# First attention of a two-block transformer kernel: probabilities turned on VectorE, values as 32-row tiles

## The chip, the cores and the metric

The kernel runs on one NeuronCore of one Trainium2 chip. The metric is the time of the whole program in device microseconds, smaller is better. TensorE is written PE in the rows, VectorE DVE, ScalarE ACT, GpSimd POOL, SyncE SP.

## What is computed

Two transformer blocks over 512 tokens of width 1024, all in float32. The change lies in the mixer of the first block: sixteen query heads in two groups of eight, each group with one key and value head of width 64, over a band of two blocks of 128 tokens, with a learned sink in each softmax. Its output is gated, added to a gated pooling mixer, and projected.

```python
def swa_sink_attention(q, k, v, sinks):
    qb = q.reshape(B, nb, BLOCK, N_KV_HEADS, GQA_GROUP, HEAD_DIM)     # nb = 4 blocks of 128
    kb, vb = band(k), band(v)                                         # the block before and the block itself
    s = jnp.einsum('bnqhgd,bnkhd->bhgnqk', qb, kb, ...)
    s = jnp.where(mask, s, -jnp.inf)
    m = jnp.maximum(jnp.max(s, axis=-1, keepdims=True), sink)
    p = jnp.exp(s - m)
    denom = jnp.sum(p, axis=-1, keepdims=True) + jnp.exp(sink - m)
    probs = (p / denom).astype(v.dtype)
    out = jnp.einsum('bhgnqk,bnkhd->bnqhgd', probs, vb)
...
        a = pool_mixer(u_pool, w_pool[l], pool_scale[l])
        b = swa_sink_attention(q, k, v, sinks[l])
        x = x + (g_pool * a + g_attn * b) @ w_out[l]
```

The mask leaves the 128 keys up to each query. The first block of 128 queries has no block before it, so it needs only 128 keys; the other three need 256.

## The kernel before

Activations lie transposed, features on the 128 partitions and tokens along the free axis. All weights come as one stream of units, each 1024 x 128. SyncE loads a unit into one of two `raw` buffers; GpSimd splits it into a high part and a low part in the fp32r format (`split`, L486 and L494; a few high parts are made by ScalarE, `weight_high`). Four pairs of buffers `w_hi`, `w_lo` go round. A tile of a projection (`tile`, L1102) is 24 matmuls of 128 x 128 weights by 512 tokens: eight key tiles, three products each (high by high, high by low, low by high). A buffer is free again when its unit's tile is done (`unit_done`). Each engine runs its own program in order; semaphores tie them together.

The first block goes: input projections of the pooling part, K and V, Q; then the attention loop, into which the 16 gate projections are woven; then the output projection (`U_OUT`, eight units); then the feed-forward part.

V arrives transposed in `vT` and is turned by four TensorE transposes (L1251) in round t = 3 of the Q projections, into `vtok` (tokens on partitions). In that stage VectorE scales each tile (`scaled_in`, L1915) and applies the rotation (`qk`), and last_window and window_parts of the pooling part stand between.

The attention loop has 16 steps n. Step n handles four heads of block `blk = n // 4`; two successive steps make up the eight heads of group `g = n // 2 % 2`. The work of a step:

- TensorE: `scores(n + 2)` (L1283, two 64-row tiles side by side, into PSUM banks 2 and 3), `turn(n)` (L1293, profiled under the helper's line L1167: 128 x 128 transposes of the probabilities), `gate(n + 2)` (one projection tile, L1102), `values(n)` (L1303, two column tiles of 64 side by side).
- VectorE: `scaled_in` of the gate tile (L1915), `masked_max(n + 2)` (L2025 to L2040: adds the mask, reduces, takes in the sink), `normalise(n + 1)` (L2048 to L2052: adds the sink's share, reciprocal, multiplies the probabilities), `attn_out` for every second step (L2067: multiplies the values' result by the gate), `gate_pool` from step 7 (L2058).
- ScalarE (all its operations are recorded at L581): `turned(n)` copies the transposed probabilities from PSUM to `pT`, `gate(n + 1)` takes tanh of the gate tile, `exps(n + 2)` exponentiates the four heads and sums them.

So the softmax of a step is made two steps ahead, and TensorE covers it with the gate tile. The last two steps have no gate tile.

After the loop VectorE adds pooling and attention (`mixed`, L2101), ScalarE makes the high part (`high(1, REAL)`) and VectorE the low part (L1852) into `h_hi5` and `h_lo5`, one key tile after the other. TensorE takes the first two tiles of the output projection together by key tile (`tile_pair`, L1121), then five single tiles (L1102), then the last in two halves of 256 tokens (`tile_sides`, L1176). VectorE adds each finished tile to the residual (L2123).

`gbuf` is the memory of `g_hi` and `g_lo`, which the pooling part uses up to `pooled(1)` and the feed-forward part uses later.

Of the kernel before, what the change touches and what calls it, by code (L numbers as in the profile page):

```python
# [17 lines left out]
P = 128  # L18
# [7 lines left out]
T = 512  # L26
# [111 lines left out]
def build(nc, w_stream, w_ba, x_t, vec, cst, cst1, cst2, pos, out):  # L138
    ctx = ExitStack()
    with ctx:  # L140
# [58 lines left out]
        vtok = ar(NB, P)  # L199
# [4 lines left out]
        vT_r = arena_r[:, ar.at:ar.at + T]  # L204
        vT = ar(T)
# [5 lines left out]
        GA = arena[:, mid:mid + 8 * T].rearrange("p (a b) -> p a b", b=T)  # L211
        ar.at = mid + 8 * T
        sm_r = [arena_r[:, ar.at + 1024 * n:ar.at + 1024 * (n + 1)].rearrange("p (a b) -> p a b", b=256) for n in range(2)]
        sm = [ar(4, 256), ar(4, 256)]
        pT = ar(2, 512)
# [43 lines left out]
        def area(x, *shape):  # L259
# [58 lines left out]
            "s_ready s_read mx_ready exp_ready p_ready pT_ready pT_copied pv_done o_read "  # L318
# [51 lines left out]
        def sum_banks(d):  # L370

            return (0, 0, 0, 0, 2, 4, 0, 2)[d]

# [203 lines left out]
        def _(act):  # L577
# [83 lines left out]
            a(vT, ps[:, 1, :], ACT.Copy).then_inc(S["tile_read"], 1)  # L661
            weight_high(13)
            for t in range(1, 9):
# [20 lines left out]
            def gate(i):  # L684
                act.wait_ge(S["in_scaled"], 10 + i + 1)
                if i == 0:
                    act.wait_ge(S["qk_dve"], 9)
                    act.wait_ge(S["v_turned"], 1)
# [12 lines left out]
            def exps(n):  # L701
                s = sm[n % 2] if n >= 4 else sm[n % 2][:, :, P:2 * P]
# [382 lines left out]
        def _(pe):  # L1085
# [8 lines left out]
            def tile(u, i, dst, pieces=None):  # L1094

                a_hi, a_lo = (h_hi, h_lo) if pieces else (h_hi5, h_lo5)
# [72 lines left out]
            def tile_sides(u, banks, between=None):  # L1169

                pe.wait_ge(split_done[u % 4], rounds(u))
                hi, lo = w_hi[u % 4], w_lo[u % 4]
                for c, side in enumerate(sides):
                    for k in range(KT):
                        for n, (w, h) in enumerate(((hi, h_hi5), (hi, h_lo5), (lo, h_hi5))):
# [66 lines left out]
            for t in range(1, 9):  # L1242
                pe.wait_ge(S["tile_read"], t + 8)
                tile(U_Q + t - 1, 0, [ps[:, (9 + t) % 2, :]])
                if t == 3:
# [4 lines left out]
                    for b in range(NB):  # L1250
                        last = turned_into(ps[:, 7, b * P:(b + 1) * P], vT_r[:, b * P:(b + 1) * P])  # L1251
# [22 lines left out]
            def scores(n):  # L1274
                blk, g, half = n // 4, n // 2 % 2, n % 2
# [11 lines left out]
            def turn(n):  # L1287
                blk = n // 4
                pe.wait_ge(S["p_ready"], n + 1)
                wait(pe, S["pT_copied"], n)  # L1290
                for kb in range(0 if blk else 1, 2):
                    for m in range(4):
                        last = turned_into(ps[:, 4 + kb, m * P:(m + 1) * P], sm_r[n % 2][:, m, kb * P:(kb + 1) * P])  # L1293
                last.then_inc(S["pT_ready"], 1)

            def values(n):
                blk, g, half = n // 4, n // 2 % 2, n % 2
                pe.wait_ge(S["pT_copied"], n + 1)
                wait(pe, S["o_read"], n // 2 - 1)
                kbs = range(0 if blk else 1, 2)  # L1300
                for kb in kbs:
                    for par in range(2):
# [1333 lines left out]
```

## Time and profile before

| | |
|---|---|
| time, median of 3 runs | 1422.29 us (1421.27 to 1424.07) |
| span of the profiled execution | 1420.3 us |
| TensorE busy | 1364.4 us, 96% |
| VectorE busy | 712.4 us, 50% |
| ScalarE busy | 442.0 us, 31% |
| GpSimd busy | 903.1 us, 64% |
| attention loop | about 140 to 270 us of the span |

The median lies 2.0 us over the span of the profiled execution. A record of a matmul lasts longer than its share of the engine, since matmuls overlap; the time between two starts is what one costs. A float32 matmul leaves two records, an fp32r matmul one. "idle before" names the wait ahead of an instruction and what released it. The granted clock (PEclk) is a share of 2.4 GHz.

### The profile page before, as it was taken

The numbers are of one execution on the slowest core, as the hardware profiler recorded it, in microseconds if no ns is written. First come the engines' busy times: TensorE is split into PE (matmuls) and PEld (weight loads), VectorE is DVE, ScalarE is ACT, GpSimd is POOL, SyncE is SP. The second block draws the span as 40 slices with busy tenths as digits, with TensorE's granted clock in tenths as the row PEclk, the third lists the DMA queues.
The fourth block names the chain that finished last, engine by engine and source line by source line (L and its number), as shares of the span: only waits on it lengthen the run. The fifth ranks groups of instructions, "written<-read, shape, count | busy, mean of one in ns | idle before, by whom it ended". The sixth has DMA issues, their size and how long they took to land. (4 is left out here: it accounts for less than half of the span.)

```text
span 1420.3 us, 20890 instructions
## 1 busy us (share of the span) xinstructions
PE 1364.4 (96%) x7495; PEld 1113.6 (78%) x7495; DVE 712.4 (50%) x1147; ACT 442.0 (31%) x888; POOL 903.1 (64%) x1043
## 2 busy tenths in 40 slices
PE   7999999999999999999899999889989999999996
PEld 5877777688888888888778886649788888888884
DVE  7888767744444445113578875685554111211113
ACT  3344544422212122111345445634433111111111
POOL 6856655377777777876465753414367767687772
PEclk9999999999999999999999999999999999999998
DMA  5321311133323232322121111000022332233221
GB/s 195 107 87 60 105 60 60 45 104 107 103 89 103 89 103 89 104 91 101 45 78 57 48 59 60 16 1 2 30 89 82 111 97 95 89 104 99 93 89 60
DMA packets 31888, 113.78 MB, mean 80 GB/s; under 512 B 3536, under 2 KB 3920, under 8 KB 31696
## 3 DMA queue, kind: packets, MB, share of 16 engines
q1 hardware_dynamic: 31680, 112.72, 24.1%
q8 instruction: 43, 0.70, 0.2%
q14 instruction: 21, 0.17, 0.0%
q10 hardware_dynamic: 144, 0.18, 0.0%
HBM read 110.79 MB, written 2.10 MB: 79 GB/s over the span
## 5 line engine op out<-in xcount | busy, mean ns | idle before, releaser
L494 POOL TENSOR_TENSOR w_lo<-raw,w_hi 128x256 fp32r<-128x256 f32 (+1 forms) x804 | 649.7, 838 | 42.4 <-ACT w_hi L581 26.5
L486 POOL TENSOR_SCALAR w_hi<-raw 128x1024 fp32r<-128x1024 f32 (+1 forms) x188 | 202.6, 1078 | 382.9 <-issue 340.8
L1102 PE MATMUL ps<-h_hi,w_hi 128*128 128x512 f32 x912 | 362.0, 397 | 0.8 <-POOL w_lo L494 0.7
L1102 PE MATMUL ps<-h_lo,w_hi 128*128 128x512 f32 x912 | 355.2, 390 | 0.0
L1102 PE MATMUL ps<-h_hi,w_lo 128*128 128x512 f32 x912 | 355.1, 389 | 0.0
L1102 PEld LDWEIGHTS ps<-h_hi,w_hi 128*128 128x128 f32 x912 | 171.2, 188 | 40.3 <-issue 3.2
L1102 PEld LDWEIGHTS ps<-h_lo,w_hi 128*128 128x128 f32 x912 | 171.2, 188 | 37.7 <-issue 3.0
L1102 PEld LDWEIGHTS ps<-h_hi,w_lo 128*128 128x128 f32 x912 | 171.2, 188 | 35.9
L581 ACT ACTIVATE arena<-ps 128x512 f32<-128x512 f32 (+6 forms) x194 | 90.4, 501 | 228.0 <-PE ps L1167 74.7
L581 ACT ACTIVATE arena<-arena 128x512 f32<-128x512 f32 (+6 forms) x194 | 102.4, 531 | 174.7 <-DVE arena L2552 119.2
L2166 DVE TENSOR_TENSOR g_lo<-arena,g_hi 128x512 fp32r<-128x512 f32 x54 | 47.0, 879 | 210.6 <-ACT g_hi L581 210.6
L1365 PE MATMUL ps<-g_hi,w_hi 128*128 128x512 f32 x368 | 143.2, 389 | 0.0
L1365 PE MATMUL ps<-g_lo,w_hi 128*128 128x512 f32 x368 | 143.2, 389 | 0.0
L1365 PE MATMUL ps<-g_hi,w_lo 128*128 128x512 f32 x368 | 143.2, 389 | 0.0
L581 ACT ACTIVATE arena<-ps,V 128x512 f32<-128x512 f32 (+2 forms) x115 | 80.8, 720 | 198.8 <-DVE ps L2150 128.8
L581 ACT ACTIVATE g_hi<-arena 128x512 fp32r (+1 forms) x54 | 33.4, 630 | 217.1 <-PE ps L1365 201.8
L2552 DVE SCALAR_TENSOR_TENSOR arena<-ps,arena 128x512 f32<-128x512 f32 x32 | 21.7, 690 | 119.9 <-PE ps L1102 113.7
L1365 PEld LDWEIGHTS ps<-g_hi,w_lo 128*128 128x128 f32 x368 | 69.1, 188 | 14.4
L1365 PEld LDWEIGHTS ps<-g_lo,w_hi 128*128 128x128 f32 x368 | 69.1, 188 | 14.4
L1365 PEld LDWEIGHTS ps<-g_hi,w_hi 128*128 128x128 f32 x368 | 69.1, 188 | 14.3
L2150 DVE TENSOR_TENSOR ps<-ps,arena 128x512 f32<-128x512 f32 x33 | 23.1, 699 | 102.1 <-PE ps L1102 102.1
L2298 DVE SCALAR_TENSOR_TENSOR arena<-arena,V 128x528 f32<-128x528 f32 x48 | 53.8, 1121 | 16.2 <-ACT arena L581 14.7
(308 smaller groups left out, 1989.8 us busy)
## 6 DMA issues: line engine op xcount, KB each, us to landing
raw<-in_w_stream SPq DMA_DIRECT2D x204, 512.0 KB, 3.4
out<-xT SPq DMA_DIRECT2D x8, 256.0 KB, 2.0
xT<-in_x_t SPq DMA_DIRECT2D x1, 1056.0 KB, 8.1
xT<-in_x_t SPq DMA_DIRECT2D x1, 792.0 KB, 6.0
arena<-in_cst SPq DMA_DIRECT2D x1, 528.0 KB, 4.4
C<-in_cst SPq DMA_DIRECT2D x1, 448.0 KB, 9.4
xT<-in_x_t SPq DMA_DIRECT2D x1, 264.0 KB, 3.7
arena<-in_pos SPq DMA_DIRECT2D x1, 256.0 KB, 3.6
```

The source lines that it names most:

```text
L486: pool.tensor_scalar(w_hi[j][:, k0:KT, :], raw[j % 2][:, k0:KT, :], 1.0, 1.0, ALU.mult, ALU.mult).then_inc(S["pool_step"], 1)
L494: low = pool.tensor_tensor(w_lo[j][:, k:k + n, :], raw[j % 2][:, k:k + n, :], w_hi[j][:, k:k + n, :], ALU.subtract)
L581: return nc.scalar.activation(o, i, f, **kw)
L1102: last = mm(dst[p], w[:, k, :], h[:, k, cols], start=(k == 0 and n == 0), stop=(k == KT - 1 and n == 2))
L1365: last = mm(ps[:, f, :], w[:, f, :], h[:, j, :], start=(start and n == 0), stop=(stop and n == 2), skip_group_check=True)
L2150: v.tensor_tensor(ps[:, q + 1, :], ps[:, q + 1, :], n_ri[:, 0:T], ALU.mult).then_inc(S["up_scaled"], 1)
L2166: v.tensor_tensor(g_lo[:, j, :], src[:, ds(4 * i + j), :].rearrange("p a b -> p (a b)"), g_hi[:, j, :], ALU.subtract).then_inc(S["ms_ready ...
L2298: ins = v.scalar_tensor_tensor(out=y5, in0=x5[:, d % 2, j:j + L], scalar=vcol("dconv", 12 * j + d), in1=y5, op0=ALU.mult, op1=ALU.add)
L2552: v.scalar_tensor_tensor(out=rb[:, q, :], in0=ps[:, bank, :], scalar=0.0, in1=n_ri[:, 0:T], op0=ALU.max, op1=ALU.mult).then_inc(S["relu_re ...
```

## The change

In words:

- Order: step n now handles group `n // 8`, block `n // 2 % 4`, half `n % 2` (`head_step`): first all four blocks of the first eight heads, then those of the second.
- V is written by ScalarE four times over (`vT` gets 2048 elements a partition), turned by sixteen TensorE transposes, four in each of the rounds t = 3 to 6, and copied to `vrep` in four pieces. So each strip of 32 partitions holds all values of 32 keys.
- The normalising multiplication moves from VectorE to ScalarE (`normalised`, four scaled copies); VectorE keeps the denominators.
- The probabilities are no longer turned by TensorE and copied by ScalarE. VectorE turns them in 32 x 32 blocks into `p_turned` (in `gbuf`).
- `values(k)` works on two steps at once: up to 64 matmuls of 32 rows by 64 columns with 128 moving columns, into PSUM banks 4 to 7, one bank for each strip of 32 queries. `attn_out(k)` reads the four banks with four instructions.
- `mixed` and its high and low part for key tiles 0 to 3 move into the loop (steps 10 to 14); high parts go over `GA` (`GA_r`), low parts over `U` (`U_r`), no longer to `h_hi5` and `h_lo5`.
- The output projection takes three tiles together (`out_three`), first key tiles 0 to 3, then `values(7)`, then key tiles 4 to 7; four single tiles and the last one in halves follow, with banks `f % 4`.

```diff
@@ ACT, rounds of the Q projections
-                    act.wait_ge(S["v_turned"], 1)
-                    a(vtok.rearrange("p a b -> p (a b)"), ps[:, 7, :], ACT.Copy).then_inc(S["v_ready"], 1)
+                if 3 <= t < 7:
+                    act.wait_ge(S["v_turned"], t - 2)
+                    a(vrep[:, 4 * (t - 3):4 * (t - 2), :].rearrange("p a b -> p (a b)"), ps[:, 7, :], ACT.Copy).then_inc(S["v_ready"], 1)
@@ ACT, attention loop
-            def turned(n):
-                act.wait_ge(S["pT_ready"], n + 1)
-                wait(act, S["pv_done"], n)
-                if n >= 4:
-                    a(pT[:, 0, :], ps[:, 4, :], ACT.Copy)
-                a(pT[:, 1, :], ps[:, 5, :], ACT.Copy).then_inc(S["pT_copied"], 1)
+            def normalised(n):
+                s = sm[n % 2] if head_step(n)[1] else sm[n % 2][:, :, P:2 * P]
+                act.wait_ge(S["den_ready"], n + 1)
+                b = 16 * (n % 2)
+                for m in range(4):
+                    last = a(s[:, m, :], s[:, m, :], ACT.Copy, scale=small[:, b + 8 + m:b + 9 + m])
+                last.then_inc(S["p_ready"], 1)
+
+            def mixed_high(f):
+                act.wait_ge(S["hn_ready"], f + 1)
+                a(GA_r[:, f, :], n_h[:, f % 2, 0:T], ACT.Copy).then_inc(S["hi_ready"], 1)
 
             exps(0)
             pooled_out(1)
             for n in range(16):
-                turned(n)
+                normalised(n)
                 if n == 0:
                     exps(1)
                 if 1 <= n < 15:
                     gate(n + 1)
+                if 11 <= n < 15:
+                    mixed_high(n - 11)
                 if n < 14:
                     exps(n + 2)
-            high(1, REAL)
+            for f in range(4, KT):
+                mixed_high(f)
@@ PE, attention loop
-            def values(n):
...
+            def values(k):
+
+                g, blk, _ = head_step(2 * k)
+                pe.wait_ge(S["pt_ready"], 2 * k + 2)
+                wait(pe, S["o_read"], k)
+                for kb in range(0 if blk else 4, 8):
+                    for c in range(4):
+                        for par in range(2):
+                            last = mm(ps[64 * par:64 * par + 64, 4 + c, 0:P], vrep[q32(c), 4 * (blk - 1) + kb, 64 * g:64 * g + 64],
+                                      p_turned[q32(c), k % 2, :, 2 * par:2 * par + 2, 32 * kb:32 * kb + 32],
+                                      start=(kb == (0 if blk else 4)), stop=(kb == 7))
+                last.then_inc(S["pv_done"], 1)
@@
             for n in range(16):
                 if n < 14:
                     scores(n + 2)
-                turn(n)
-                if n < 14:
                     gate(n + 2)
-                if n == 0:
+                if n == 1:
                     pe.wait_ge(S["pm_read"], 8)
-                values(n)
+                if n % 2 and n < 15:
+                    values(n // 2)
             pe.wait_ge(S["tile_read"], 34)
-            tile_pair(U_OUT, 1, [[ps[:, 0, :]], [ps[:, 1, :]]])
...
+            pe.wait_ge(S["s_read"], 16)
...
+            out_three(range(4))
+            values(7)
+            out_three(range(4, KT))
@@ DVE, attention loop
-            def normalise(n):
+            def denominators(n):
                 b = 16 * (n % 2)
-                lo = 0 if n >= 4 else P
-                s = sm[n % 2][:, :, lo:256]
                 dve.wait_ge(S["exp_ready"], n + 1)
                 den = small[:, b + 8:b + 12]
                 step(v.tensor_tensor(den, den, small[:, b + 12:b + 16], ALU.add))
                 step.settle()
-                step(v.reciprocal(den, den))
-                step.settle()
-                v.tensor_tensor(s, s, den.unsqueeze(2).to_broadcast([P, 4, 256 - lo]), ALU.mult).then_inc(S["p_ready"], 1)
+                v.reciprocal(den, den).then_inc(S["den_ready"], 1)
+
+            def turn(n):
+
+                g, blk, half = head_step(n)
+                lo = 0 if blk else P
+                dve.wait_ge(S["p_ready"], n + 1)
+                wait(dve, S["pv_done"], n // 2 - 1)
+                if n == 0:
+                    product(dve, U_PM + 1)
+                v.transpose(p_turned[:, n // 2 % 2, half, :, lo:256], sm[n % 2][:, :, lo:256]).then_inc(S["pt_ready"], 1)
@@
+            def attn_out(k):
+
+                g, blk, _ = head_step(2 * k)
+                dve.wait_ge(S["pv_done"], k + 1)
+                dve.wait_ge(S["tile_read"], 18 + 4 * g + 4)
+                for c in range(4):
+                    c0 = blk * P + 32 * c
+                    ga = GA[:, 4 * g:4 * g + 4, c0:c0 + 32]
+                    ins = v.scalar_tensor_tensor(out=ga, in0=ga, scalar=1.0, in1=ps[:, 4 + c, 0:P].rearrange("p (a b) -> p a b", b=32),
+                                                 op0=ALU.add, op1=ALU.mult)
+                ins.then_inc(S["o_read"], 1)
@@
             masked_max(0)
-            normalise(0)
+            denominators(0)
             masked_max(1)
             for n in range(16):
+                turn(n)
                 if 1 <= n < 15:
                     scaled_in(U_GATE + n + 1, (n + 1) % 2)
-                if n == 6:
-                    attn_out(3)
+                if n % 2 == 0 and 2 <= n < 15:
+                    attn_out(n // 2 - 1)
                 if n < 14:
                     masked_max(n + 2)
                 if n < 15:
-                    normalise(n + 1)
...
+                    denominators(n + 1)
                 if 7 <= n < 15:
                     gate_pool(n - 7)
...
+                if 10 <= n < 14:
+                    mixed(n - 10)
+                if 11 <= n < 15:
+                    mixed_low(n - 11)
+            attn_out(7)
+            for f in range(4, KT):
+                mixed(f)
+                if f > 4:
+                    mixed_low(f - 1)
+            mixed_low(KT - 1)
```

## Rows read from the trace of the kernel before

**Rows 1.** Stages: us from:to, length, busy us of each engine, PEclk, DMA share, GB/s

```profile
180.00:220.00 40.00, 39.76 (x224) 29.47 (x222) 28.80 (x50) 18.65 (x60) 18.74 (x23) 1.00 0.21 66
266.00:268.00 2.00, 0.88 (x8) 0.74 (x8) 1.97 (x4) 1.02 (x3) 0.61 (x1) 0.97 0.08 8
268.00:270.00 2.00, 1.88 (x8) 0.77 (x8) 1.83 (x4) 1.15 (x3) 0.00 (x0) 0.50 0.64 254
270.00:272.00 2.00, 2.00 (x8) 1.65 (x7) 1.97 (x5) 0.63 (x1) 0.00 (x0) 0.67 0.00 0
```

**Rows 2.** TensorE timeline, one step with 256 keys: start us, duration us, engine, line

```profile
227.32 1.08 PE L1303 MATMUL ps<-arena 128*64 128x256 f32 x8
228.33 1.13 PE L1283 MATMUL ps<-arena 64*128 64x256 f32 x8
229.40 0.88 PE L1167 MATMUL ps<-ident_r,arena_r 128*128 128x128 f32 x8
230.12 0.47 PE L1102 MATMUL ps<-h_hi,w_hi 128*128 128x512 f32 x1
...
235.74 1.08 PE L1303 MATMUL ps<-arena 128*64 128x256 f32 x8
```

**Rows 3.** TensorE timeline, values and transposes of a step with 128 keys

```profile
161.66 0.65 PE L1303 MATMUL ps<-arena 128*64 128x256 f32 x4
162.25 1.13 PE L1283 MATMUL ps<-arena 64*128 64x256 f32 x8
163.31 0.53 PE L1167 MATMUL ps<-ident_r,arena_r 128*128 128x128 f32 x4
```

**Rows 4.** TensorE timeline, end of the loop and start of the output projection

```profile
264.09 1.08 PE L1303 MATMUL ps<-arena 128*64 128x256 f32 x8 [1.17 <-ACT arena L581]
266.07 0.88 PE L1167 MATMUL ps<-ident_r,arena_r 128*128 128x128 f32 x8 [0.89 <-DVE arena L2052]
268.12 1.98 PE L1303 MATMUL ps<-arena 128*64 128x256 f32 x8 [1.17 <-ACT arena L581]
270.03 0.80 PE L1121 MATMUL ps<-h_hi,w_hi 128*128 128x512 f32 x1
...
281.92 0.50 PE L1102 MATMUL ps<-h_hi,w_hi 128*128 128x512 f32 x1
```

**Rows 5.** TensorE: second attention's values (timeline), and 32x32 matmuls by line

```profile
806.22 1.46 PE L1496 MATMUL ps<-arena 128*64 128x128 f32 x20
...
L1666 PE MATMUL ps<-arena,hbuf x128: 191/191/212, 953.9 to 955.1; 32*32 32x32 f32 x128
```

**Rows 6.** VectorE timeline: scaled_in, masked_max from its first to its last instruction

```profile
213.02 0.69 DVE L1915 TENSOR_TENSOR ps<-ps,arena 128x512 f32<-128x512 f32 x1
213.62 1.21 DVE L2025 TENSOR_TENSOR arena<-ps,band 128x1024 f32<-128x1024 f32 x1
...
216.52 0.16 DVE L2040 TENSOR_TENSOR arena<-arena,V 128x4 f32<-128x4 f32 x1
```

**Rows 7.** ScalarE timeline: pooled_out(1), first and last of exps, eight scaled copies

```profile
146.31 2.43 ACT L581 ACTIVATE arena<-ps,V 128x512 f32<-128x512 f32 x4 [1.87 <-PE ps L1265]
...
216.71 0.51 ACT L581 ACTIVATE arena<-arena 128x256 f32<-128x256 f32 x1 [1.58 <-DVE arena L2040]
...
218.70 0.19 ACT L581 ACTIVATE arena<-arena 128x4 f32<-128x4 f32 x1
...
312.33 3.31 ACT L581 ACTIVATE h_hi<-xT,V 128x256 fp32r<-128x256 f32 x8 [1.52 <-PE ps L1176]
```

**Rows 8.** VectorE by line: duration ns min/median/max of transposes; a PSUM copy, mean ns

```profile
L2372 DVE STREAM_TRANSPOSE arena<-hbuf x4: 692/702/707, 918.1 to 920.3; 32x512 f32<-32x512 f32 x4
...
L2380 DVE STREAM_TRANSPOSE arena<-arena x1: 2081/2081/2081, 921.3 to 921.3; 128x1024 f32<-128x1024 f32 x1
...
L2292 DVE COPY arena<-ps 128x128 f32<-128x128 f32 x16 | 4.6, 286 | 0.4 <-PE ps L1496 0.4
```

**Rows 9.** V's transposes on TensorE, and VectorE's wait in round 7

```profile
87.09 0.86 PE L1167 MATMUL ps<-ident_r,arena_r 128*128 128x128 f32 x4
87.79 1.09 PE L1235 MATMUL ps<-arena,C 128*128 128x512 f32 x2
...
113.40 0.70 DVE L1915 TENSOR_TENSOR ps<-ps,arena 128x512 f32<-128x512 f32 x1 [0.39 <-PE ps L1102]
```

More of the change, by code:

```diff
@@ L203, in build @@
         W0, W1 = ar(2, L), ar(2, L)
-        vT_r = arena_r[:, ar.at:ar.at + T]
-        vT = ar(T)
+        vT, vT_r = (x[:, AC - 4 * L:AC - 4 * L + 16 * P].rearrange("p (b c k) -> p b c k", c=4, k=32) for x in (arena, arena_r))
         sqb, qgb = ar(2, T), ar(2, T)
@@ L1092, in unit, with tile @@
                 last.then_inc(unit_done[u % 4], 1)
-            def tile(u, i, dst, pieces=None):
-                a_hi, a_lo = (h_hi, h_lo) if pieces else (h_hi5, h_lo5)
+            def tile(u, i, dst, parts=None, pieces=None):
+                a_hi, a_lo = parts or ((h_hi, h_lo) if pieces else (h_hi5, h_lo5))
                 def work(hi, lo):
@@ L1249, in _ @@
                     pe.wait_ge(S["tile_read"], 10)
-                    for b in range(NB):
-                        last = turned_into(ps[:, 7, b * P:(b + 1) * P], vT_r[:, b * P:(b + 1) * P])
+                if 3 <= t < 7:
+                    wait(pe, S["v_ready"], t - 3)
+                    for b in range(4):
+                        last = turned_into(ps[:, 7, b * P:(b + 1) * P], vT_r[:, 4 * (t - 3) + b, :, :].rearrange("p c k -> p (c k)"))
                     last.then_inc(S["v_turned"], 1)
@@ L1285, in scores @@
                 last.then_inc(S["s_ready"], 1)
[L1287 to L1294, printed above, removed]
-            def values(n):
[L1297 to L1302, printed above, removed]
-                        last = mm(ps[64 * par:64 * par + 64, 6 + n // 2 % 2, 256 * half:256 * half + 256],
-                                  vtok[:, blk - 1 + kb, 64 * g:64 * g + 64], pT[:, kb, 256 * par:256 * par + 256],
-                                  start=(kb == kbs[0]), stop=(kb == 1))
+            def values(k):
[8 more added lines that the diff above has]
+                                      start=(kb == (0 if blk else 4)), stop=(kb == 7))
                 last.then_inc(S["pv_done"], 1)
@@ L1323, in _, with out_three @@
                     scores(n + 2)
-                turn(n)
-                if n < 14:
                     gate(n + 2)
-                if n == 0:
+                if n == 1:
                     pe.wait_ge(S["pm_read"], 8)
-                values(n)
+                if n % 2 and n < 15:
+                    values(n // 2)
             pe.wait_ge(S["tile_read"], 34)
-            tile_pair(U_OUT, 1, [[ps[:, 0, :]], [ps[:, 1, :]]])
-            for f in range(1, KT):
-                if f > 1:
-                    pe.wait_ge(S["x_ready"], f - 1)
-                if 1 < f < KT - 1:
-                    tile(U_OUT + f, 0, [ps[:, f % 2, :]])
-            tile_sides(U_OUT + KT - 1, (1, 3))
+            pe.wait_ge(S["s_read"], 16)
+            def out_three(ks):
+                for k in ks:
+                    pe.wait_ge(S["h_ready"], parts_before(1) + k + 1)
+                    for e in range(3):
+                        if k == 0:
+                            pe.wait_ge(split_done[(U_OUT + e) % 4], rounds(U_OUT + e))
+                        hi, lo = w_hi[(U_OUT + e) % 4], w_lo[(U_OUT + e) % 4]
+                        for m, (w, x) in enumerate(((hi, GA_r[:, k, :]), (hi, U_r[:, k, REAL]), (lo, GA_r[:, k, :]))):
+                            last = mm(ps[:, e, :], w[:, k, :], x, start=(k == 0 and m == 0), stop=(k == KT - 1 and m == 2))
+                        if k == KT - 1:
+                            last.then_inc(unit_done[(U_OUT + e) % 4], 1)
+            out_three(range(4))
+            values(7)
+            out_three(range(4, KT))
+            for f in range(3, KT):
+                wait(pe, S["x_ready"], f - 3)
+                if f < KT - 1:
+                    tile(U_OUT + f, 0, [ps[:, f % 4, :]], (GA_r, U_r[:, :, REAL]))
+            pe.wait_ge(S["x_ready"], KT - 2)
+            tile_sides(U_OUT + KT - 1, (1, 3), (GA_r, U_r[:, :, REAL]))
             def up(i):
@@ L1426, in wide @@
                     pe.wait_ge(S["bat_ready"], 2)
-                tile(u, 0, [ps[:, 2 * (n % 2), :]], [REAL])
+                tile(u, 0, [ps[:, 2 * (n % 2), :]], pieces=[REAL])
             def k2_side(t):
@@ L2018, in masked_max @@
             def masked_max(n):
+                g, blk, half = head_step(n)
                 b = 16 * (n % 2)
-                lo = 0 if n >= 4 else P
+                lo = 0 if blk else P
                 s = sm[n % 2][:, :, lo:256]
                 dve.wait_ge(S["s_ready"], n + 1)
-                wait(dve, S["pT_ready"], n - 1)
+                wait(dve, S["pt_ready"], n - 1)
                 m = band[:, lo:256].unsqueeze(1).to_broadcast([P, 4, 256 - lo])
```

72 lines of the change are left out of this document (31 added, 41 removed).

## The prediction

> **What bounds the kernel now.** I read the page first (TensorE 96% of the span), then the stages. In 180 to 220 us TensorE is busy 39.76 of 40 us, VectorE 28.80, ScalarE 18.65 [rows 1]: TensorE sets the pace of the attention loop. The TensorE timeline of one step (four heads, 256 keys) gives its period: values at 227.32, scores at 228.33, transposes at 229.40, the gate tile from 230.12, the next values at 235.74 [rows 2]. That is 8.42 us: values 1.01, scores 1.07, transposes 0.72, gate 5.62. In a step with 128 keys the values take 0.59 (161.66 to 162.25), and I take half, 0.37, for its transposes [rows 3]. At the end no gate tile is left to cover the softmax: three waits of 1.17, 0.89 and 1.17 us, the last values take 1.91 us instead of 1.01, and the output projection starts at 270.03 [rows 4]. Its first pair of tiles ends at 281.92, and six tiles of 5.44 us (24 matmuls of 0.227) follow.
>
> The question is what the period of a step becomes when TensorE sheds work and the other two engines get an order of their own.
>
> **Part 1, TensorE's own work.** Gone: the transposes, 12 x 0.72 + 4 x 0.37 = 10.1 us, and the values, 12 x 1.01 + 4 x 0.59 = 14.5 us. New: eight values blocks, six of 64 matmuls and two of 32, each matmul 32 rows x 64 columns with 128 moving columns. The nearest size is second attention's values: 10 matmuls of 128 columns in 1.46 us, two column tiles side by side; less 0.16 for the last one's way out, 0.26 us for one tile's matmul [rows 5]. With eight tiles side by side, 64 matmuls are eight such slots, 2.1 us; no concurrency beyond two gives 64 x 0.13 = 8.3 us. The nearest in concurrency are the 32x32 matmuls: 128 records (64 matmuls) start within 1.1 us, four tiles at a time [rows 5]. The diff's order (four row strips, two column halves, then the next key block) names eight different tiles in a row, so I take 2.2 us (1.2 for the half block). TensorE alone would then need 2 x (1.07 + 5.62) + 2.2 = 15.6 us for two steps, not 16.84.
>
> Those records start some 9 ns apart. The Trainium skill says in TensorE: Matmul & The Clock Gate, Wait — 56ns, not 53.3ns?, that start to start never drops below about 25 ns; by that the 128 records of a block would take 3.2 us, 1.0 us over my figure. The trace disagrees, at least for 32x32 tiles.
>
> **Part 2, the loop of VectorE and ScalarE.** This carries the forecast. ScalarE's new order is normalised(n), gate(n+1), exps(n+2); VectorE's is turn(n), scaled_in(n+1), attn_out, masked_max(n+2), denominators(n+1). So turn(n+1) waits for normalised(n+1), which stands on ScalarE behind exps(n+2), which waits for masked_max(n+2), which stands on VectorE behind turn(n). Each step runs this whole ring, and nothing in it overlaps:
> masked_max 3.06 us (213.62 to 216.68) [rows 6]; exps 2.18 (216.71 to 218.89) [rows 7]; normalised, four scaled copies of 256 columns, by the row of eight such copies in 3.31 us 0.40 each and 0.10 at the end, 1.70 [rows 7]; turn 1.16; scaled_in 0.60 (213.02 to 213.62) [rows 6]; three handoffs of 0.03. The transpose of 1024 elements is bounded by 2.08 us (strided on both sides) and by 0.70 for 512 with runs of 32; the diff's reads and writes are contiguous, nearest to the second, which makes 1.24 with 0.08 overlapped [rows 8]. Sum 8.79 us. Every second step adds attn_out, four instructions of 128 elements at 0.29 [rows 8] less overlap: 0.85. Two steps take 18.4 us, against 16.84 now and TensorE's own 15.6. TensorE waits some 2.8 us in every two steps, and VectorE becomes part of the bound though it is busy less than TensorE. gate_pool, mixed, mixed_low and the denominators lie in VectorE's wait for ScalarE (3.9 us): nothing. gate and mixed_high lie on ScalarE beside masked_max: nothing. A slower values block is covered up to those 2.8 us in two steps.
>
> The walk. turn(0) comes after pooled_out(1) (146.31 + 2.43 [rows 7]) and a normalised of 128 columns (1.26, an estimate: 0.11 less for each copy): 150.0. Up to turn(15) the ring holds: masked_max 2 to 15, 12 x 3.06 + 2 x 1.86 = 40.4; exps, 12 x 2.18 + 2 x 1.74 = 29.7; normalised 1 to 15, 12 x 1.70 + 3 x 1.26 = 24.2; turns 0 to 14, 11 x 1.16 + 4 x 0.62 = 15.2; scaled_in 14 x 0.60 = 8.4; attn_out 7 x 0.85 = 6.0; the first attn_out waits 0.6 for gate 3; the last denominators 0.4; handoffs 1.3. Together 126.2 (the half sizes 1.86, 1.74 and 0.62 are the same rows at half the elements). turn(15) starts at 276.2.
>
> **Part 3, the tail.** The output projection now takes three tiles together, and its first half (key tiles 0 to 3) only waits for gate 15 and its reader: turn(14) + 2.4 us, or 273.8. Before it TensorE idles some 7 us, since after values(6) it has no work. 36 matmuls, 8.16 us, to 281.9; values(7) 2.2, to 284.1; attn_out 0.85, mixed 0.60, the high part 0.63, the low part 0.69 and handoffs 0.13, to 287.0; 36 matmuls more, to 295.2. Before, three tiles were done at 281.92 + 5.44 = 287.36 [rows 4]. So +7.8 us. The five tiles that follow have the old price; POOL's splits for them (3.9 us each) begin when the first of the three tiles is done and stay ahead of 5.44 us tiles.
>
> **Part 4, turning the values earlier.** Sixteen transposes instead of four: three batches more, each up to 0.70 us (87.09 to 87.79) and at least 0.37 [rows 9]. VectorE waits for TensorE's tile in that stage up to the seventh round (0.39 us at 113.40) [rows 9], so a later tile is passed on: 0 to 2.1, I take +1.6. ScalarE's wider copy of V (2048 elements) and three copies more lie in its waits of 3 us a round: nothing.
>
> **Part 5, the clock.** At 266 to 268 the granted clock is 0.97 and at 268 to 270 it is 0.50 (1.2 GHz), right after the three waits, and 0.67 in the next 2 us [rows 1]; the last values and the first projection matmuls pay for it. The old fall cost 0.9 us in the values (1.91 against 1.01 [rows 2, 4]) and 1.0 in the pair (11.89 us for 48 matmuls against 10.88), 1.9 together. The wait of 7 us before the projection is longer than those three together, so I count one fall at 1.9. The wait of 2.9 us before the second half may bring another, 0 to 1.9: half of it. Falls inside the loop are covered by the 2.8 us. Sum +2.9.
>
> **The sum.** +7.8 + 1.6 + 2.9 = +12.3 us. The profiled execution has a span of 1420.3, the median is 2.0 over it: 1432.6 in the profile, 1434.6 in the median.
>
> **The rivals.**
> A, faster: TensorE stays the bound. For it: VectorE (28.80) and ScalarE (18.65) have room in 40 us [rows 1]. Then -10.1 - 14.5 + (6 x 2.2 + 2 x 1.2) = -9.0, the three waits -3.2, the slow clock -1.9, Part 4 +1.6: -12.5, 1409.8. It decides as soon as the ring takes less than 7.8 us a step instead of 9.2. Against it: none of the ring's terms is shorter in any row, and the order is in the diff. 0.09.
> B, the transposes take 2.08 us: 11 x 0.84 + 4 x 0.33 = +10.6 more, 1445. 0.12.
> C, the change doesn't do what it says: the 32-row tiles don't overlap beyond the two column halves. Two steps then take 13.4 + 8.3 = 21.7 us on TensorE, 3.3 over the ring, five times, and 6 more in the last block: about +22 more, 1457. At four tiles side by side (4.2 us) the loop still hides it and the last block adds 2.0. 0.07.
> D, within 0.2% (1419.4 to 1425.1; about the least that a measurement tells from no change): the clock never falls, the transposes of V are hidden and attn_out's four instructions cost as much as the old one: +7.8 - 2.5 = +5.3, still 1427.6. It would need 2.5 us more than that. 0.03.
>
> **How the numbers follow.** Forecast 0.69, A 0.09, B 0.12, C 0.07, D 0.03. Ends of the forecast: low +5.3 with 0.5 off for faster values, 1427; high: V turned +0.5, clock +1.0, attn_out 4 x 0.29 +2.2, values at 3.4 us +1.2: 1439.5. B is taken in up to 1446 and the room between: 1427 to 1446 holds 0.81. Faster 0.09, same 0.03, slower 0.88.
>
> **What would show it.** After: VectorE's transposes of 1024 elements at about 1.24 us and each following a ScalarE copy; waits on VectorE for ScalarE of 2 to 3.5 us a step; waits on ScalarE for the masked maximum; two steps 18.4 us apart; TensorE's share in the loop near 85%; values blocks of 2.2 us; a TensorE wait of 7 us before the projection with the clock at 0.50 behind it. I am wrong if TensorE has no waits in the loop (A), if the transposes are near 2 us (B) or a values block above 4 us (C).

## The result, and the profile after

The changed kernel takes 1447.54 us (median of 4 runs, 1442.41 to 1448.68) against 1422.95 us before (4 runs, 1421.27 to 1424.07): a ratio of 1.0173, with a 95% interval of 1.0160 to 1.0186. The forecast was 1434.6 us with a range up to 1446.0. The direction was right, the size was half of what came: +12.3 us forecast, +24.6 us measured. The profiled execution of after has a span of 1445.5 us, where the sum said 1432.6.

First the stages, as in [rows 1]: us from:to, length, busy us of each engine, granted clock, DMA share, GB/s.

```profile
180.00:220.00 40.00, 35.61 (x422) 27.79 (x428) 25.29 (x46) 18.16 (x58) 15.96 (x21) 0.98 0.18 54
284.00:288.00 4.00, 2.31 (x6) 1.83 (x7) 3.35 (x11) 2.80 (x6) 0.00 (x0) 0.50 0.00 0
288.00:292.00 4.00, 4.00 (x13) 3.22 (x12) 1.03 (x1) 0.00 (x0) 0.00 (x0) 0.65 0.00 0
300.00:304.00 4.00, 2.22 (x5) 1.82 (x6) 3.64 (x7) 1.86 (x3) 0.00 (x0) 0.63 0.00 0
304.00:308.00 4.00, 4.00 (x11) 3.05 (x10) 1.27 (x2) 1.92 (x2) 0.00 (x0) 0.51 0.01 4
```

TensorE, 39.76 of 40 us busy in the loop before, is busy 35.61 now. What it waits for (engine, line, waited for, us in total, times, longest), in 100 to 320 us of after:

```profile
PE ps L1299 <- DVE arena L2050: 13.8, 8, 3.4
PE ps L1349 <- ACT arena L584: 8.3, 1, 8.3
PE ps L1349 <- DVE arena_r L2114: 3.1, 1, 3.1
PE ps L1311 <- DVE gbuf L2083: 2.9, 4, 1.5
```

The scores wait for masked_max (L2050 is its first instruction), the values for the turning (L2083), the projection for gate 15 and then for the low part of the fifth key tile. VectorE waits in its turn for ScalarE:

```profile
DVE gbuf L2083 <- ACT arena L584: 38.4, 15, 3.6
```

The parts of the forecast, by line on VectorE (count | busy us, mean ns | idle before), and the values blocks and the tail in TensorE's timeline (start, duration):

```profile
L2083 DVE STREAM_TRANSPOSE gbuf<-arena 128x1024 f32<-128x1024 f32 x12 | 15.0, 1246 | 31.2 <-ACT arena L584 31.2
L2063 DVE TENSOR_SCALAR arena<-arena 128x4 f32<-128x4 f32 x16 | 7.3, 456 | 0.5
L2061 DVE TENSOR_TENSOR arena<-arena,V 128x4 f32<-128x4 f32 x16 | 6.9, 430 | 0.5
L2065 DVE TENSOR_TENSOR arena<-arena,V 128x4 f32<-128x4 f32 x16 | 5.5, 342 | 0.5
```

```profile
202.28 2.10 PE L1311 MATMUL ps<-gbuf,arena 32*64 32x128 f32 x128 [1.46 <-DVE gbuf L2083]
204.31 0.72 PE L1299 MATMUL ps<-arena 64*128 64x128 f32 x8
...
285.69 1.22 PE L1349 MATMUL ps<-arena_r,w_hi 128*128 128x512 f32 x2 [8.28 <-ACT arena L584]
...
296.53 2.10 PE L1311 MATMUL ps<-gbuf,arena 32*64 32x128 f32 x128
...
301.78 1.22 PE L1349 MATMUL ps<-arena_r,w_hi 128*128 128x512 f32 x2 [3.14 <-DVE arena_r L2114]
...
312.99 0.62 PE L1115 MATMUL ps<-arena_r,w_hi 128*128 128x512 f32 x2
```

Here stand the transpose at 1.246 us (forecast 1.24), the values block at 2.03 us from start to start of what follows (2.2), the wait before the projection at 8.28 us (7) with the clock at 0.50 behind it, and the second wait at 3.14 us (2.9). Three projection tiles are done at 312.99; before they were done at 287.36 [rows 4]. That is 25.6 us of shift, so the whole loss lies ahead of this point.

What the forecast did not have is in the three groups of 128x4 instructions. Each takes 0.16 to 0.17 us when nothing disturbs it, and 0.34 to 0.46 us on the mean here. One step of after shows how. VectorE:

```profile
192.75 1.21 DVE L2050 TENSOR_TENSOR arena<-ps,band 128x1024 f32<-128x1024 f32 x1
193.99 1.22 DVE L2053 TENSOR_REDUCE arena<-arena 128x4 f32<-128x1024 f32 x1
195.25 0.50 DVE L2061 TENSOR_TENSOR arena<-arena,V 128x4 f32<-128x4 f32 x1
195.78 0.67 DVE L2063 TENSOR_SCALAR arena<-arena 128x4 f32<-128x4 f32 x1
196.49 0.65 DVE L2065 TENSOR_TENSOR arena<-arena,V 128x4 f32<-128x4 f32 x1
```

and GpSimd at the same time:

```profile
193.87 1.04 POOL L489 TENSOR_SCALAR w_hi<-raw 128x1024 fp32r<-128x1024 f32 x1 [4.82 <-issue]
195.00 2.82 POOL L497 TENSOR_TENSOR w_lo<-raw,w_hi 128x256 fp32r<-128x256 f32 x4
```

GpSimd splits the next weights in five instructions of 0.70 to 1.04 us. A small VectorE instruction that falls among them ends about when the running GpSimd instruction does. masked_max takes 4.4 us here (192.75 to 197.14) instead of the 3.06 of [rows 6]. The add from PSUM and the reduction beside it keep their 1.21 and 1.22 us. Two full steps, from one turning to the next but one, take 18.9 to 20.2 us, where the forecast had 18.4.

### The profile page after: what moved, and what is told of

Its sections match the earlier page's. It is cut to its first block and busy times, and to the rows that moved or that the text cites. A ratio compares the mean times of both kernels' runs of the same rounds, so it can differ in the third digit from the quotient of the medians.

```text
span 1445.5 us, 22303 instructions
## 1 busy us (share of the span) xinstructions
PE 1365.9 (94%) x8179; PEld 1118.1 (77%) x8179; DVE 717.7 (50%) x1171; ACT 454.0 (31%) x927; POOL 897.6 (62%) x1043
## 5 line engine op out<-in xcount | busy, mean ns | idle before, releaser
L1115 PE MATMUL ps<-h_hi,w_hi 128*128 128x512 f32 x872 | 348.4, 400 | 1.1 <-POOL w_lo L497 1.1
L1115 PE MATMUL ps<-h_lo,w_hi 128*128 128x512 f32 x872 | 341.1, 391 | 0.0
L1115 PE MATMUL ps<-h_hi,w_lo 128*128 128x512 f32 x872 | 340.9, 391 | 0.0
L1115 PEld LDWEIGHTS ps<-h_hi,w_hi 128*128 128x128 f32 x872 | 164.6, 189 | 43.4 <-issue 7.5
L1115 PEld LDWEIGHTS ps<-h_lo,w_hi 128*128 128x128 f32 x872 | 164.6, 189 | 36.7 <-issue 3.0
L1115 PEld LDWEIGHTS ps<-h_hi,w_lo 128*128 128x128 f32 x872 | 164.6, 189 | 34.5
L584 ACT ACTIVATE arena<-arena 128x256 f32<-128x256 f32 (+5 forms) x258 | 126.5, 516 | 192.2 <-DVE arena L2588 119.2
L584 ACT ACTIVATE arena<-ps 128x512 f32<-128x512 f32 (+6 forms) x169 | 77.9, 494 | 187.3 <-PE ps L1180 37.6
L2334 DVE SCALAR_TENSOR_TENSOR arena<-arena,V 128x528 f32<-128x528 f32 x48 | 53.7, 1120 | 16.1 <-ACT arena L584 14.7
```

Of the source, the lines that this page charges most:

```text
L584: return nc.scalar.activation(o, i, f, **kw)
L1115: last = mm(dst[p], w[:, k, :], h[:, k, cols], start=(k == 0 and n == 0), stop=(k == KT - 1 and n == 2))
L2334: ins = v.scalar_tensor_tensor(out=y5, in0=x5[:, d % 2, j:j + L], scalar=vcol("dconv", 12 * j + d), in1=y5, op0=ALU.mult, op1=ALU.add)
```

## The experiments

The theory: the loop is set by the circle of Part 2 (turn, masked_max, exps, normalised, turn), and it is longer than forecast because GpSimd's split stretches the small instructions of masked_max, which are part of the circle. Rivals: TensorE itself is slower than its rows of work say (32-row tiles, clock); the split has nothing to do with it; the tail is more than forecast for a reason of its own.

**e1_den_first: the circle cut by order alone**

```diff
 # ScalarE
+            normalised(0)
+            exps(1)
             for n in range(16):
-                normalised(n)
-                if n == 0:
-                    exps(1)
                 if 1 <= n < 15:
                     gate(n + 1)
+                if n < 15:
+                    normalised(n + 1)
...
 # VectorE
+                if n < 15:
+                    denominators(n + 1)
                 if n < 14:
                     masked_max(n + 2)
-                if n < 15:
-                    denominators(n + 1)
```

> One edit of order in the kernel after, nothing else: VectorE makes denominators(n+1) before masked_max(n+2) instead of behind it, and ScalarE does normalised(n+1) before exps(n+2). The probabilities of step n+1 are then ready before VectorE is through with masked_max(n+2), and the circle turn(n), masked_max(n+2), exps(n+2), normalised(n+1), turn(n+1) is cut. Theory (the loop is set by this circle, and TensorE waits for it): a step falls from 9.0 us to TensorE's own 7.7 to 7.8 us, the VectorE waits for ScalarE ahead of the turning (38 us in all) nearly vanish, the first half of the out projection starts 15 to 22 us earlier than its 285.7 us, and the whole comes to about 1428 us (1421 to 1434). Rival (TensorE itself is slower with the 32-row blocks, by tiles that do not overlap or by the clock): the order of the two vector engines changes nothing on TensorE, and the time stays at 1445 to 1449 us.

Measured: 1415.82 us, ratio to before 0.9954 (0.9940 to 0.9968). That is 31.7 us less than after, 5 us below the range that was expected, and faster than the kernel before. Its loop, from the stages:

```profile
180.00:220.00 40.00, 40.00 (x432) 31.57 (x431) 32.13 (x66) 24.54 (x82) 20.42 (x27) 1.00 0.21 67
```

TensorE is busy 40.00 of 40 us; the first half of the projection starts at 255.50 instead of 285.69, behind 0.81 us of waiting instead of 8.28. No work was taken away: the small instructions of masked_max are still stretched, to 0.27 to 0.29 us on the mean, and the denominators' add to 0.51. The order alone had cost 31.7 us, and the rival in which TensorE's own work is the cause is out. The profiled executions are 34.8 us apart. 27.1 of that lie between turn(0) and turn(15) (107.88 us instead of 134.93), 5.4 in the tail, where 2.3 and 1.4 us are a clock that falls less, 1.5 ahead of turn(0), where the clock of after had fallen and that of e1_den_first had not, and 0.8 behind the three tiles.

**e4_split_small: GpSimd's part in the circle**

```diff
-            rep(pool, U_UP // 4, split, HIGH_ROUNDS)
+            rep(pool, 9, lambda i: split(i, None, P if isinstance(i, int) else 4), HIGH_ROUNDS)
+            with pool.Fori(9, U_UP // 4, 1) as i:
+                split(i)
 # in split(i, held, w): the operands become w_hi[j][..., 0:w], raw[...][..., 0:w], w_lo[j][..., 0:w]
```

The kernel leaves out most of the split weights of 14 gate units.

> The kernel after, with GpSimd's weight split in weight units 20 to 35 cut to 4 of 128 columns of each tile (the rest of the split weights of 14 gate units are left out, so most of the gates' products are not the reference's); every wait and every other instruction stays. Theory (the circle is stretched by the small VectorE instructions of masked_max, which take 0.5 to 1.0 us instead of 0.16 while GpSimd's split runs): the groups of 128x4 instructions fall from 0.43, 0.46, 0.34 and 0.22 us to 0.16 us, a step falls from 9.0 to 9.2 us to the forecast's 8.5 to 8.8, and the whole to about 1438.5 us (1436 to 1442), which is 9 us below the kernel after and still above the kernel before. Rival (the stretch is not GpSimd's, or lies off the path): 1445 to 1449 us.

Measured: 1433.88 us, ratio 1.0087 (1.0070 to 1.0104), 13.7 us less than after and 2 us below the range that was expected. The run is its own control, since the full split comes back at 234.5 us. Without it (VectorE's timeline; line 2052 is the first instruction of masked_max, 2063 to 2067 are its small ones, 2085 is the turning):

```profile
183.23 1.25 DVE L2085 STREAM_TRANSPOSE gbuf<-arena 128x1024 f32<-128x1024 f32 x1 [3.55 <-ACT arena L586]
...
185.76 1.21 DVE L2052 TENSOR_TENSOR arena<-ps,band 128x1024 f32<-128x1024 f32 x1
...
188.66 0.16 DVE L2067 TENSOR_TENSOR arena<-arena,V 128x4 f32<-128x4 f32 x1
...
201.29 1.25 DVE L2085 STREAM_TRANSPOSE gbuf<-arena 128x1024 f32<-128x1024 f32 x1 [3.55 <-ACT arena L586]
```

and with it:

```profile
242.46 1.25 DVE L2085 STREAM_TRANSPOSE gbuf<-arena 128x1024 f32<-128x1024 f32 x1 [2.37 <-ACT arena L586]
...
244.21 1.21 DVE L2052 TENSOR_TENSOR arena<-ps,band 128x1024 f32<-128x1024 f32 x1
...
246.90 0.65 DVE L2065 TENSOR_SCALAR arena<-arena 128x4 f32<-128x4 f32 x1
247.59 0.64 DVE L2067 TENSOR_TENSOR arena<-arena,V 128x4 f32<-128x4 f32 x1
...
261.92 1.25 DVE L2085 STREAM_TRANSPOSE gbuf<-arena 128x1024 f32<-128x1024 f32 x1 [1.76 <-ACT arena L586]
```

masked_max takes 3.06 us in the first (185.76 to 188.82) and 4.02 in the second. Two steps, from turning to turning, take 18.06 us in the first (183.23 to 201.29; forecast 18.4) and 19.46 us in the second (242.46 to 261.92).

Not all of the gain is the circle's. The two profiled executions are 16.1 us apart: 4.05 us ahead of turn(0) (148.80 against 152.85), 7.55 between turn(0) and turn(15) (127.38 against 134.93), 3.64 from there to the three tiles, 0.9 behind them. Of the first 4.05, some 1.5 are the early fall of the clock in after. The 3.64 are the clock alone. Behind a second wait of 3.15 us it does not fall at all here:

```profile
289.34 0.74 PE L1351 MATMUL ps<-arena_r,w_hi 128*128 128x512 f32 x2 [3.15 <-DVE arena_r L2116]
...
297.75 0.62 PE L1117 MATMUL ps<-arena_r,w_hi 128*128 128x512 f32 x2
```

That is 8.41 us for the second half of the three tiles against 11.21 in after, and the first half takes 10.01 us against 10.84. So GpSimd's part in the circle is 7.6 us, and that the whole comes within 1 us of the forecast of 1434.6 is in part luck.

**e11_tail_split_small: the same cut where the circle is cut too** (its base, e5_tail, follows below)

> The kernel e5_tail with the same cut of GpSimd's split as in e4_split_small (weight units 20 to 35 are split in 4 of 128 columns only; the rest is left out, so most of the gates' products are not the reference's). The same cut took 13.7 us off the kernel after. Theory (the stretched small instructions cost time only as members of the circle): with the circle cut they lie beside TensorE's work, and at most the 1 to 3 us ahead of the loop, where TensorE waits 0.9 us for VectorE, can come back: 1409 us (1406.5 to 1411). Rival (the split slows the loop in some other way as well, through TensorE's weights or the loads): 1397 to 1401 us.

Measured: 1407.88 us, ratio 0.9902 (0.9879 to 0.9924), 2.6 us less than e5_tail. The small instructions of masked_max fall to 0.16 to 0.17 us as well, and next to nothing comes of it: turn(0) starts 2.6 us earlier (148.76 against 151.38), and from there to turn(15) it is 107.13 us against 106.94 in e5_tail. In this loop the contention costs time only through the circle.

**e8_values_twice and e9_tail_values_twice: who has slack**

```diff
-                for kb in range(0 if blk else 4, 8):
+                for kb in 2 * list(range(0 if blk else 4, 8)):
```

The same line was changed in the kernel after and in e5_tail.

> The kernel after, with each block of values multiplied twice over (the second pass starts the sums anew): TensorE has 2.05 us more work per pair of steps (1.2 us at the two half-size blocks), 14 to 15 us in all eight blocks. Theory (the loop waits for the circle through VectorE and ScalarE, and TensorE has 2 to 3 us of idle time in each pair of steps there): the seven blocks inside the loop cost next to nothing, values(7) stands on the path and costs its 2.05 us; the whole comes to 1449.5 us (1448 to 1453). Rival (TensorE sets the pace): 1461 to 1463 us.

> The kernel e5_tail with each block of values multiplied twice over, the same addition that cost the kernel after nothing. Theory (with the circle cut TensorE sets the pace of the loop): the 14 us of added matmuls come out in full, 1424 us (1421 to 1426). Rival (VectorE, 80 to 90% busy there, sets the pace and TensorE has slack): 1411 to 1415 us.

Measured: after with doubled values 1445.30 us (ratio 1.0154, 1.0135 to 1.0173), not slower than after and below the range expected; e5_tail with doubled values 1428.54 us (1.0047, 1.0029 to 1.0065), 18.1 us slower than e5_tail and above the range expected. The added matmuls are 12.4 us and not the 14 of the expectations: a block of 64 matmuls grows from 2.03 to 3.80 us, one of 32 from 1.14 to 2.03. In after those within the loop are free (turn(0) to turn(15) 135.17 us against 134.93), and the wait of 8.28 us before the projection shrinks to 4.83. values(7), behind the loop, is not free: it brings its 1.8 us and a gap of 1.17. The clock gives that back, since the second half takes 9.71 us instead of 11.21 and the early fall is missing (turn(0) starts at 151.20 instead of 152.85). Once the circle is cut, the added matmuls cost their full time. What lies above that comes at least in part with gaps in and behind the doubled streams, for which the profile names nothing that TensorE waits for (the waits of e9_tail_values_twice; the scores have 2.5 us of the same kind, and e8_values_twice has 5.7 us in all):

```profile
PE ps L1312 <- issue: 3.6, 3, 1.4
```

How much of the median they make is open, for the profiled execution of e9_tail_values_twice is the slowest of its four, 4.8 us above the median.

**e6_fill: the clock behind the first wait**

```diff
-            pe.wait_ge(S["tile_read"], 34)
             pe.wait_ge(S["s_read"], 16)
+            for _ in range(34):
+                mm(ps[:, 3, :], ident_r[:], h_hi5[:, 0, :], start=True, stop=True)
+            pe.wait_ge(S["tile_read"], 34)
```

> The kernel after, with 34 matmuls of 128x512 (7.7 us) into an unused PSUM bank where TensorE waits 8.3 us for the last gate ahead of the out projection; nothing else is changed. Theory (after the wait the first half of the out projection runs at a granted clock of 0.50 to 0.65 and takes 10.8 us instead of 8.3): with the wait filled the clock stays at 1.00, the first half takes 8.3 to 8.5 us and the whole comes to 1445 us (1443.5 to 1446.5); the fall after the second wait (3.1 us) stays. Rival (the fall comes whatever TensorE did before, or only moves): 1447 to 1448 us and a first half of 10.8 us.

Measured: 1445.58 us, ratio 1.0160 (1.0141 to 1.0178), 2.0 us less than after. The two intervals overlap, so the times alone do not show a gain. The trace is clear:

```profile
277.36 8.00 PE L1339 MATMUL ps<-h_hi,ident_r 128*128 128x512 f32 x34
285.30 0.73 PE L1351 MATMUL ps<-arena_r,w_hi 128*128 128x512 f32 x2
...
293.80 2.10 PE L1311 MATMUL ps<-gbuf,arena 32*64 32x128 f32 x128
```

The first half takes 8.50 us (285.30 to 293.80) at a granted clock of 1.00, against 10.84 in after (285.69 to 296.53) at 0.50 and 0.65.

**e10_tail_alone and e5_tail: the second wait**

```diff
 # TensorE
-            out_three(range(4))
+            out_three(range(2))
             values(7)
-            out_three(range(4, KT))
+            out_three(range(2, KT))
...
 # VectorE
-                turn(n)
+                if n < 15:
+                    turn(n)
...
+                if n == 14:
+                    turn(15)
                 if 7 <= n < 15:
                     gate_pool(n - 7)
```

> The kernel after with the tail's edit alone (turn(15) ahead of the gate and mixing work of VectorE's step 14, values(7) behind the second key tile), the order of the loop as in the kernel after. Theory (in the kernel after the wait of 3.1 us between the halves and the clock of 0.63 and 0.51 behind it are the price of the tail's order, apart from the circle in the loop): both go, worth 3.1 us and 1.5 to 2.5 us, and the whole comes to 1442.5 us (1441 to 1444.5); the first half still starts behind a wait of 8 us and at a clock near 0.50. Rival (turn(15) is now waited for by VectorE, so that the gates and parts behind it come later and the gain is used up): 1446 to 1449 us.

> The kernel e1_den_first, with turn(15) put ahead of the gate and mixing work of VectorE's step 14 and values(7) put behind the second key tile of the out projection's first half instead of behind the fourth. Theory (the wait of 3.1 us between the halves stands because attn_out(7), mixed(4) and mixed_low(4) can only start once values(7) is through, and the granted clock of 0.61 behind it costs 1.2 us more): VectorE does these three beside key tiles 2 and 3, no wait and no fall are left, and the whole comes to 1411.5 us (1409.5 to 1413.5), some 4.3 us below e1_den_first. Rival (another wait takes its place, at values(7) for turn(15) or at the later key tiles for mixed_low): 1414 to 1417 us.

Measured: on the kernel after 1442.88 us (ratio 1.0140, 1.0120 to 1.0161), 4.7 us less; on e1_den_first 1410.46 us (0.9921, 0.9904 to 0.9938), 5.4 us less. In both the wait of 3.14 us is gone. In e10_tail_alone the first wait is still 8.3 us; the clock behind it comes back and stays:

```profile
288.00:292.00 4.00, 4.00 (x11) 3.12 (x10) 2.42 (x3) 0.66 (x2) 0.00 (x0) 0.54 0.00 0
292.00:296.00 4.00, 4.00 (x137) 3.23 (x136) 0.60 (x3) 0.00 (x0) 0.00 (x0) 1.00 0.02 4
```

e5_tail is the version that beats both kernels: 12.5 us under before, 37 under after, with the change's own parts and no work left out. Its steady pair of steps:

```profile
223.87 1.13 PE L1300 MATMUL ps<-arena 64*128 64x256 f32 x8
...
239.39 1.13 PE L1300 MATMUL ps<-arena 64*128 64x256 f32 x8
```

15.52 us for two steps. Part 1 had said 15.6 for TensorE alone, and rival A 1409.8 us for the whole.

What the clock takes behind the second wait is not a fixed price. That wait is 3.14 to 3.15 us in five profiled executions, and the second half behind it takes 11.21 us in after, 11.17 in e6_fill, 9.79 in e1_den_first, 9.71 in e8_values_twice and 8.41 in e4_split_small.

**e7_parts: a slower pace of the projection's matmuls**

```diff
+        def part_at(f):
+            return (h_hi5[:, f, :], h_lo5[:, f, :]) if f >= 4 else (GA_r[:, f, :], U_r[:, f, REAL])
```

All writers and readers of the parts take their operands from it, and ScalarE waits for gate tile 15 before it writes key tile 4.

> The kernel e5_tail, with the parts of key tiles 4 to 7 written to the tiles h_hi5 and h_lo5 (free by then) instead of into arena_r in place of the gates and of U. Theory (three matmuls of the projection take 0.695 us instead of 0.680 because their moving operands come from arena_r): groups of three on key tiles 4 to 7 take 0.680 us and those on key tiles 0 to 3 still 0.695 us, worth 0.5 us in all, which the times do not resolve: 1411 us (1409 to 1413.5). Rival (the slower pace is that of this stage, whatever is read): 0.695 us for all of them.

Measured: 1410.24 us (0.9915, 0.9899 to 0.9932), no difference from e5_tail. Three matmuls on arena_r take 0.695 us. On h_hi and h_lo they take 0.680 us in most of the second half of the three tiles, but 0.69 us in the single tiles, where key tiles 0 to 3 still come from arena_r (2.77 us for the twelve from 288.33 to 291.10). So neither side holds as put: the operand's place alone is not the cause. What is, stays open. It is 0.1 us a tile.

## Why the prediction was right in its mechanism and wrong in its size

By the sum's own steps, in the profiled executions:

| step | forecast us | after us | difference |
|---|---|---|---|
| turn(0) starts | 150.0 + 1.6 | 152.85 | +1.3 |
| turn(0) to turn(15) | 126.2 | 134.93 | +8.7 |
| turn(15) to three tiles done | 19.0 + 2.9 | 25.21 | +3.3 |
| three tiles done | 299.7 | 312.99 | +13.3 |

The times behind this point are 0.4 us shorter than in the sum, which gives the 12.9 us between 1432.6 and 1445.5.

**Part 1 held.** Values 2.03 us instead of 2.2. Two steps of TensorE's own work are 15.52 us in e5_tail instead of 15.6. The 128 records of a block start 16 ns apart. The Trainium skill's floor of about 25 ns from start to start (TensorE: Matmul & The Clock Gate, Wait — 56ns, not 53.3ns?) would have made it 3.2 us, as the prediction read it, by records; the trace disagrees with that reading for 32x64 tiles too. By matmuls, of two records each, they start 32 ns apart, which lies above the floor. The 32x32 matmuls of [rows 5] are below it either way, 64 of them in 1.1 us.

**Part 2, the step that failed: masked_max at 3.06 us.** The circle is shown: cut by order the kernel takes 31.7 us less, and TensorE work put into the loop costs nothing until it is cut. Its terms apart from one were right, or a little long (18.06 against 18.4 us in two steps without the split). The wrong one is masked_max, priced from the one instance of [rows 6], in which GpSimd was idle. Summed over masked_max 2 to 15, its three small instructions take 10.4 us more than undisturbed; 1.7 us of that are made up by the other terms, 8.7 us are left. The cut of the split in e4_split_small gives back 7.6 us between the same two points. The profile of before had a warning in its groups (count | busy us, mean ns):

```profile
L2040 DVE TENSOR_TENSOR arena<-arena,V 128x4 f32<-128x4 f32 x16 | 4.4, 275 | 0.5
L2038 DVE TENSOR_SCALAR arena<-arena 128x4 f32<-128x4 f32 x16 | 4.2, 264 | 0.5
L2036 DVE TENSOR_TENSOR arena<-arena,V 128x4 f32<-128x4 f32 x16 | 3.8, 235 | 0.6
```

The instance in [rows 6] has 0.16 us for L2040 where the mean is 0.275. Before, VectorE had time to spare and the excess was free. But the means would have covered only 4.0 of the 10.4 us (0.284 us in each of 14 steps), and the instance was a fair one: in before masked_max 1 to 4 are stretched, at 148 to 167 us, and the eleven from 174 us on have 0.16 to 0.17 us. What changed is when the two meet. A split takes 3.9 us in after and up to 4.4 in before. In before, from 174 us on, the small instructions begin 4.6 to 7.7 us after it does, behind its end (one step of before):

```profile
210.69 1.05 POOL L486 TENSOR_SCALAR w_hi<-raw 128x1024 fp32r<-128x1024 f32 x1 [3.92 <-issue]
...
216.12 0.16 DVE L2036 TENSOR_TENSOR arena<-arena,V 128x4 f32<-128x4 f32 x1
```

In after, from 176 us on, they begin from 0.1 us before its start to 3.4 us after it in nine steps of twelve (193.87 and 195.25 above), and are stretched in these nine alone. GpSimd may start on a unit when TensorE has finished a gate tile, and in after TensorE then waits for the first instruction of masked_max. That the circle brings the two together is read from the trace; no run changed it by itself.

The Trainium skill names this in SBUF — State Buffer, Who interferes with whom: GpSimd and VectorE share a port pair as an exclusive lock, taken by a VectorE instruction with two SBUF inputs or in a two-port mode, and whoever comes second is blocked for the other's whole instruction, while a reduction never is. The traces agree: L2061 and L2065 (two SBUF inputs) are stretched and end with a GpSimd instruction, L2063 (a TENSOR_SCALAR) too, though no view shows in which mode it runs, the add from PSUM stays at 1.21 us and the reduction at 1.22. The page would have priced a small instruction that meets the split at up to a whole GpSimd instruction; the rows of GpSimd give 0.70 to 1.04 us for that.

**Part 3 held in its times**: the first wait 8.28 us (7), the second 3.14 (2.9), turn(14) to the projection 2.6 (2.4). It treated the second wait as given. e5_tail shows that it was a matter of where values(7) stands.

**Part 4** was +1.6, and pooled(0) starts 0.94 us later than before (129.77 against 128.83): three batches of transposes more, each 0.29 us from its start to that of what follows (94.13 to 94.42). turn(0) is 1.3 us late all the same, behind two things: a clock of 0.80 and 0.77 at 128 to 136 us, with which pooled(0) takes 7.14 us instead of 5.53, and masked_max(1), stretched by 1.4 us, which turn(0) stands behind. That fall comes and goes: e6_fill and e10_tail_alone have it and e8_values_twice does not, though all three are the kernel after up to there, and before and e1_den_first don't have it either.

**Part 5, the clock, was too small**: 2.9 in all, against 2.5 for the first half (10.84 us against 8.34, 36 matmuls at 0.2317) and 2.9 for the second (11.21 against 8.34), 5.4 together. Both figures are whole ones, since the 287.36 us of before, with which the sum compares, hold the old fall. e6_fill gives back 2.3 of the first by filling the wait, e10_tail_alone removes the second with its wait. A fall was priced at what it had cost before, and the second at half a fall; in the profiled execution of after each was longer than the old one. That is one draw of several: the same second wait cost from nothing to 2.9 us in the five executions named above, 1.7 on their mean, where the sum had 0.95 and a ceiling of 1.9.

**The rivals.** B and C are out by their durations (1.246 and 2.03 us). A failed where it was said to: the circle takes more than 7.8 us a step. With the circle cut by e1_den_first and the tail put in order it is nearly the time measured, 1410.46 against 1409.8, though that is another kernel than the one A spoke of. No rival covered what happened: B and C moved a term that the change adds, and none asked whether a term kept from before could grow.

## What to carry to other kernels

When work goes from the engine that bounds a loop to engines with much idle time, follow the order in which these run their steps: a chain that leads from one step round to the next sets the period whatever the busy shares say, and a change of order can cut it for nothing (31.7 us here). Price the members of such a chain by the range of their groups in the stage, and not by one clean instance. Ask what will run on the other engines at their new place in time, because delays that were free before now count in full, and a new order can make two engines meet that had missed each other. Where TensorE waits ahead of a long stretch of matmuls, look first for work that can stand there, since the wait can be paid for a second time in the clock (from nothing to 2.9 us here). Compare profiled executions stage by stage, for such falls differ between executions that run the same code up to there, by as much as a small experiment gains.

## What the runs showed of the hardware that I had not expected

- A 128x4 VectorE instruction takes 0.16 us alone and mostly 0.4 to 1.0 us beside GpSimd's 128x1024 and 128x256 fp32 instructions, if it has two SBUF inputs or is a TENSOR_SCALAR. The reciprocal of 128x4 keeps its 0.178 us and the reduction its 1.22.
- Tiles of 32 rows and 64 columns run side by side well: 128 records of 128 fp32 columns in 2.03 us, 256 in 3.80.
- In and behind streams doubled to 256 records TensorE shows gaps of 0.7 to 1.5 us of which the profile names no cause.
- Behind the same wait of 3.14 to 3.15 us the granted clock fell long enough to cost 2.8 to 2.9 us in two executions, 1.4 to 1.5 in two, and not at all in one, set against 8.34 us for 36 matmuls.
- The projection's matmuls of 512 columns start 0.2317 us apart in after and 0.2267 before, at the same granted clock of 1.00. The cause is open.
